# One weight load placed between the transfers of a bias table, and three VectorE steps in another order

## The reference

```python
h = rms_norm(x, mix_norm_g)
proj = h @ w_in                        # 1024 x 3072, twelve weight chunks
oa = moba_attention(qa, ka, va, table_a)      # 8 heads; a bias by token distance is added to the logits
ob = diff_attention(qb, kb, vb, table_b, ...) # 4 heads of two maps each
mixed = concat(rms_norm(oa), ob)
x = x + mixed @ w_out                  # four weight chunks
x = x + memory_cross_attention(x, mem, ...)   # begins with h @ w_cq, and k = m @ w_ck
...
# second block, layer 0: attention beside a causal convolution of three taps
conv = cb * causal_depthwise_conv(cc * cx, conv_w)
x = x + concat(attn, conv) @ w_out_2          # "hy_out"
```

## Time and profile before

| | |
|---|---|
| three runs, median (lowest to highest) | 1052.43 us (1050.34 to 1052.84) |
| the profiled execution's own time | 1052.22 us |
| its span, first to last instruction | 1050.4 us |
| TensorE busy in the span | 1040.6 us (99%) |
| VectorE busy | 863.1 us (82%) |
| ScalarE busy | 671.6 us (64%) |
| mean rate of the DMA engines | 178 GB/s |
| granted TensorE clock, mean | 0.998 of full |

### The profile page before, as it was taken

One profiled execution on the slowest core, in us unless ns is written; L12 is line 12 of the kernel. 1 busy time (PEld: TensorE's weight loads), 2 busy tenths in 40 slices (PEclk: granted clock), 3 DMA queues, 4 the chain that ended last, 5 costly groups with the idle time before them and its releaser, 6 DMA issues.

```text
span 1050.4 us, 19060 instructions
## 1 busy us (share of the span) xinstructions
PE 1040.6 (99%) x7330; PEld 963.6 (92%) x7330; DVE 863.1 (82%) x1083; ACT 671.6 (64%) x952; POOL 2.7 (0%) x8
## 2 busy tenths in 40 slices
PE   8999999999999999999999999999999999999998
PEld 7888999898888999999899999999899889999998
DVE  6789886687877856898998888798998899888786
ACT  7566655566555447666787667675546678667673
POOL 0000000000000000000000000000000000000000
PEclk9999999999999999999999999999999999999999
DMA  9952454344555564634646555454333465555541
GB/s 337 237 194 84 147 208 161 130 174 166 193 200 184 182 237 158 191 124 154 209 180 216 193 183 192 163 212 168 123 121 121 166 235 174 189 209 198 195 147 60
DMA packets 30529, 186.91 MB, mean 178 GB/s; under 512 B 3735, under 2 KB 6520, under 8 KB 8840
## 3 DMA queue, kind: packets, MB, share of 16 engines
q1 hardware_dynamic: 29896, 185.05, 50.6%
q10 hardware_dynamic: 576, 1.05, 0.3%
HBM read 183.96 MB, written 1.34 MB: 176 GB/s over the span
## 4 chain that ended last, share of the span: by engine, by line
PE 86%; DVE 7%; DMA 3%; ACT 3%; issue 1%; ACTq 0%; DVEq 0%
PE g L531 56%; PE d L531 29%; DVE w_lo L1544 3%; DMA raw<-weights 2%; ACT w_hi L1054 2%; DMA x<-x_t 1%; PE d L534 1%; DVE b_both L1548 1%; DVE x L1541 1%; DVE sq_sum L1541 0%; DVE conv_out L1541 0%; DVE a_both L1548 0%; DVE scores L1548 0%; DVE row_max L1631 0%; DVE mem_k_lo L1544 0%
## 5 line engine op out<-in xcount | busy, mean ns | idle before, releaser
L1544 DVE TENSOR_TENSOR w_lo<-raw,w_hi 128x2048 fp32r<-128x2048 f32 (+1 forms) x175 | 389.4, 2227 | 61.7 <-ACT w_hi L1054 61.4
L531 PE MATMUL g<-a_both,w_hi 128*128 128x256 f32 (+1 forms) x1568 | 407.2, 335 | 3.2 <-DVE w_lo L1544 3.2
L1054 ACT ACTIVATE w_hi<-raw 128x2048 fp32r<-128x2048 f32 (+1 forms) x174 | 324.7, 1871 | 62.9 <-PE d L531 39.1
L531 PE MATMUL g<-a_both,w_lo 128*128 128x256 f32 x1136 | 320.1, 282 | 0.0
L531 PEld LDWEIGHTS g<-a_both,w_hi 128*128 128x128 f32 x1568 | 267.7, 191 | 36.0 <-DVE w_lo L1544 5.3
L531 PEld LDWEIGHTS g<-a_both,w_lo 128*128 128x128 f32 x1136 | 216.6, 191 | 0.1
L531 PE MATMUL g<-b_both,w_hi 128*128 128x256 f32 (+1 forms) x720 | 168.2, 311 | 0.4 <-DVE b_both L1544 0.4
L531 PE MATMUL d<-hid_hi,w_hi 128*128 (+1 forms) x528 | 146.0, 277 | 0.0
L531 PE MATMUL d<-hid_lo,w_hi 128*128 (+1 forms) x528 | 145.9, 276 | 0.0
L531 PE MATMUL d<-hid_hi,w_lo 128*128 (+1 forms) x528 | 145.9, 276 | 0.0
L531 PE MATMUL g<-b_both,w_lo 128*128 128x256 f32 x448 | 126.2, 282 | 0.0
(11 more groups left out here) (334 smaller groups left out, 1436.8 us busy)
## 6 DMA issues: line engine op xcount, KB each, us to landing
raw<-weights SPq DMA_DIRECT2D x168, 1024.0 KB, 4.8
bias_tab<-bias_dram SPq DMA_DIRECT2D x8, 192.0 KB, 10.4
x<-x_t ACTq DMA_DIRECT2D x4, 256.0 KB, 5.8
raw<-weights SPq DMA_DIRECT2D x4, 256.0 KB, 6.9
raw<-weights SPq DMA_DIRECT2D x2, 512.0 KB, 8.2
mem_t<-mem_t SPq DMA_DIRECT2D x1, 1024.0 KB, 9.0
out<-x SPq DMA_DIRECT2D x3, 256.0 KB, 2.1
hy_swap<-hy_qk SPq DMA_DIRECT2D x4, 128.0 KB, 5.9
```

The source lines that it names most:

```text
L531: return pe.matmul(out, lhsT, rhs, start=start, stop=stop, skip_group_check=True)
L1054: return act.activation(out, in_, func, **kw)
L1544: return dve.tensor_tensor(out, a, b, ALU.subtract)
```

## The change

In SP's list the load of chunk 7 goes between the third and the fourth of the eight bias transfers. On VectorE three steps move. The residue of chunk 8 is taken before the eviction of chunk 6's product, and no longer after the row maxima. The residue of `w_out`'s third chunk is taken before the residual addition begins, and no longer after its first product. In the convolution the two attention residues come after the third tap of the second pair, and no longer after its second tap. No instruction is added or taken away.

```diff
             for a in range(0, P, SKEW):
+                if a == 3 * SKEW:
+                    load(7, 7 % U)
                 skewed = bass.AP(bias_dram.tensor, P - 1 - a, ...)
                 sp.dma_start(bias_tab[a:a + SKEW], skewed).then_inc(got_bias, 16)
-            stream(7, FIRST["up0"] + U)
+            stream(8, FIRST["up0"] + U)
...
+            ahead("w_in", W_IN_Q, W_IN_Q % U)
             evict("w_in", W_IN_Q, W_IN_Q % U, pair_at(qkv, W_IN_Q), split=False)
             dve.wait_ge(got_bias, 16 * P // SKEW)
             for t, cols in score_tiles(scores, ...):
                 negate_max(scores, t, cols)
-                if t == 1:
-                    ahead("w_in", W_IN_Q, W_IN_Q % U)
             ahead("w_in", 7, 1)
...
             turned_scale(rstd_mem_tok)
-            residual("w_out", C, "cross_norm_g")
+            ahead("w_out", 0, 0)
+            residual("w_out", C, "cross_norm_g", split_first=False)
...
-                    if i == 1 and tap == 1:
+                    if i == 1 and tap == 2:
                         lo_parts(B, 0, [hy_att[:, f, :] for f in range(2)])
```

## The result

The changed kernel takes 1058.62 us (1056.11 to 1059.52, four runs) against 1051.82 us (1050.34 to 1052.84, four runs): a ratio of 1.0062, with an interval of 1.004 to 1.0084. It is slower by 6.8 us by the medians (6.5 by the ratio), where I forecast no change; it lies above my range. The profiled execution took 1056.11 us with a span of 1054.3, 3.9 longer than the span of before, so it shows 3.9 of the 6.8 us.

The account below looks back on a forecast made before the run. TensorE, busy 1040.6 of 1050.4 us, was taken as the bound, with only its waits to win. The terms +0.89 - 0.47 - 0.43 = -0.01 us gave 1052.4 us, no change, range 1049.9 to 1054.2.

Parts of the forecast that it names:

- chunk 8 where it landed before, at 50.6: the same bytes stand ahead of it: DMA queue under SP's new load order: chunk 8's landing assumed unchanged at 50.6 us; this number decides +0.89 us net.
- the 0.77 and 0.41 us that I booked as a gain: TensorE's waits before chunks 7 and 8 in the profile of before, both forecast to go.
- My own price: First scores after chunk 8's residue: each us of later landing costs one us; at 50.6, scores 1.30 us later.
- the other two edits: VectorE's moves at w_out's third chunk and in the convolution: forecast -0.47 and -0.43 us.
- The clock: Rival: TensorE's stand of 2.1 us between score matmuls lowers the granted clock, +1.3 us, giving 1053.7 us; chance 0.12.
- The chain of causes: Around chunks 7 and 8: chunk 7 early, TensorE's wait moves into its middle, some 2 us, and the 0.41 goes.
- The price one for one: First scores: each further us of chunk 8's landing costs a us; +0.89 us net at 50.6, -1.18 by 48.5.
- the second edit: Residue of w_out's third chunk before the residual addition: 0.61 us wait goes, 0.14 appears, net -0.47 us.
- the third: Attention residues after the convolution's third tap: TensorE's 0.43 us wait goes, -0.43 us, bounds 0 and -0.6.
- chunk 8 lands late: Rival: a hole in the DMA engines delays chunk 8, passed on us for us; 1 us makes 1053.4; chance 0.09.
- two mishaps: Slower than 0.3% was said to need a hole of 3.2 us or two mishaps; slower got 0.04.

Follow-up runs that it names:

- the two of the hold: Kernel before, with SP waiting for chunk 4's split between the third and fourth bias transfer, load order unchanged, run twice: 1051.93 and 1051.31 us beside 1051.74.
- lo8_only: Kernel before with only chunk 8's residue moved in front of the eviction of chunk 6's product: 1051.68 us beside 1050.46, ratio 1.0007.
- the filled kernels: Changed kernel with eight products of zeros on TensorE before the first scores, measured twice: 1053.41 and 1053.74 us, ratios 1.0025 and 1.003 to before.
- the third chip: Changed kernel and its version with zero products measured again on another chip, beside before at 1051.06 us: 1055.75 and 1053.74 us.
- wout_conv: Kernel before with only the w_out and convolution moves on VectorE: 1050.85 us beside 1050.46, ratio 1.0006.
- after_no_load: Changed kernel without SP's move of chunk 7's load: 1051.9 us beside 1051.32 for before, ratio 1.0004.
- six_between: Kernel before with chunk 6's load between the third and fourth bias transfer, run twice: 1053.88 and 1053.68 us beside 1051.74, ratios 1.0023 and 1.0026.

## Why the prediction was wrong

**The step that failed** is "chunk 8 where it landed before, at 50.6: the same bytes stand ahead of it". The same bytes stand ahead of it, and it still comes later. With the old order of loads it landed at 50.59, 50.09, 48.78 and 47.17 (mean 49.2; with the two of the hold 48.6), with the new one at 52.28, 51.10, 49.26, 51.01, 49.98, 51.31, 51.18 and 52.34 (mean 51.1): some 2 us later, with a scatter of over 1 us either way. The two groups overlap, so that this is shown for the mean and not for each execution. Bytes ahead in the queue were a bad measure of the wait. In the profiled execution it made 1.8 us of the 3.9 that I had not forecast; nearly all the rest, 2.1 us, is the clock.

**The same step hid a second fault: the execution that I summed against.** In the profile of before chunk 7 landed at 48.12. In five other executions with the old order it landed at 43.7 to 46.7, TensorE had no wait before chunks 7 and 8, and reached the scores at 53.1 to 53.6 (in `lo8_only` this is where its stand begins), not at 54.76. So the 0.77 and 0.41 us that I booked as a gain were rarely there to be had, and the stand counts from 53.4. My own price, with this put right: chunk 8 at 51.1, the scores 5.6 us later at 56.7, a stand of 3.3 us, less 0.4 us at the other two edits, makes +2.9 us without the clock, and 5.2 with a fall of 2.3 in each execution. Measured were +3.0 and +2.7 us for the filled kernels, the first of which has some 0.5 us of its own, and +4.7, +4.9 and +6.8 us for the changed kernel. Of the 2.9 us between this and my forecast 1.8 are the waits and the late start that only the summed execution had, 0.6 the landing (51.1 for 50.6, and the step from the landing to the scores), and 0.5 the two other edits. So in the runs, other than in the profile, the choice of the execution weighs more than the landing.

**The clock** was the rival that I gave 0.12, priced at 1.3 us from the narrow matmuls of 438 us. In the sum it stood at nothing. It fell in the profiled execution and cost 2.3 us. How often it falls isn't known, but the clocks of all runs bear on it: a mean of 0.9950, 0.9957 and 0.9966 over the changed kernel's 4, 7 and 12 runs, against 0.9988 and 0.9983 filled and 0.9980 to 0.9985 for before. Over 1050 us a mean clock lower by 0.0019, as on the third chip, is an estimated 2.0 us at most, since what falls into a stand costs nothing. Side by side on the third chip the fill takes 2.0 us off the median (1055.75 to 1053.74), 1.2 by the ratios and 0.6 by the mean of the runs, so the size of the share stays uncertain. The page TensorE: Matmul & The Clock Gate of the Trainium skill, in its section on why this matters for kernels, speaks against idle gaps between bursts of matmuls; the fall behind the stand of 3.92 us agrees with it, the stand of 3.07 us without one shows that a gap need not bring it.

**What was right.** The chain of causes: chunk 7 early enough for its residue (45.56 here where I wrote 41.6; 41.9 and 40.4 in two other executions), the wait moved into chunk 7 and released by `scores`, the 0.41 us before chunk 8 gone. That VectorE stood idle 4.42 us before chunk 8's residue, where I forecast 4.3, is luck: chunk 7 came 4.0 us and chunk 8 1.7 us later than forecast, and the other two executions have 5.39 and 3.81 us. The price one for one: the landing was 1.69 us later than I assumed and the scores 3.10 us later instead of 1.30, that is 1.80 more. In this one trace the second edit gave 0.41 us (4.75 down to 4.34; forecast 0.47, with a new wait of 0.19 where I expected 0.14) and the third about 0.4 (4.34 to 3.9; forecast 0.43); over all traces they are mis-sized, with 0.25 and 0.19 us. The rival "chunk 8 lands late" was right that VectorE passes a late landing on us for us, and wrong on why it is late: the engines had no hole. I let it decide only from 3.2 us; half of that and the clock together were enough, and I had set such a pair aside as two mishaps.

**What stays open.** Why chunk 8 comes later in the new order. And why the profiled execution of the changed kernel was the fastest, or nearly so, in each of its three samples (1056.11, 1052.9 and 1049.91 us against medians of 1058.62, 1056.18 and 1055.75): what the slower executions look like inside isn't seen.

**A version that beats the changed kernel** and is no slower than before is the change without VectorE's first move: 0.9993 and 0.9985 of before. Only the second interval (0.997 to 0.9999) excludes no gain, and by little.

## What to carry to other kernels

Two moves, each with no cost that the runs can tell, can cost together when each uses up the same slack: here one made a chunk late and the other made everybody wait for it, so try such edits in combination as well as alone. Don't put the split of the data that land last in front of a step on which the bounding engine waits, and don't take "the same bytes ahead" for the same landing. Before summing against one profiled execution, look whether the waits that you mean to remove are there in others too, and after the change, whether they stay away in more than one.

## What was unexpected of the hardware

- A transfer's landing scatters by over 4 us from execution to execution: chunk 7, in the old order, at 43.7 to 48.1, and chunk 8 at 46.2 to 50.6 (before, `wout_conv`, `after_no_load`, `lo8_only` and the two of the hold). In four of these six TensorE didn't wait for either.
- TensorE's clock fell to the 1.2 GHz level behind stands of 2.07, 3.92 and 5.86 us, and not behind those of 1.42, 1.50 and 3.07 us, nor behind the 2.33 and 2.52 us of `six_between`. Zero products put into the wait kept it at 2.4 GHz in both profiled executions.
